# Moving eight adaLN groups of a decoder step from the up loops to the down loops of its first feed-forward stage

## The chip, the cores and the metric

The kernel runs on one core of one Trainium2 chip. The metric is the device time of one execution in microseconds (us), as the median of several runs.

## The reference

One inference step of a one-layer decoder trunk in fp32, for 256 prompt tokens and 8 sample tokens (264 columns in all). Nine modulation vectors of 2048 come from `silu(c) @ w_ada + b_ada`, and the layer is

```
mod = silu(c) @ w_ada + b_ada                       # sh1, sc1, gt1, shm, scm, gtm, sh2, sc2, gt2
h = h + 0.5 * gt1 * swiglu(modulate(h, norm_ffn1, sh1, sc1), w_ffn1_up, w_ffn1_down)
y = mixer(modulate(h, norm_mix, shm, scm))          # gated DeltaNet and dilated window attention
h = h + gtm * y
h = h + 0.5 * gt2 * swiglu(modulate(h, norm_ffn2, sh2, sc2), w_ffn2_up, w_ffn2_down)
return rmsnorm(h, norm_final)
swiglu(x, up, down) = (silu(x @ up[:, :FF]) * (x @ up[:, FF:])) @ down      # FF = 5632
modulate(h, gain, sh, sc) = rmsnorm(h, gain) * (1 + sc) + sh
```

## The kernel before

All weights are streamed once from memory in panels of 128 partitions. An up, qkv or adaLN panel holds 16 tiles of 128x128 (1 MB); a down panel holds 11 (704 KB). SP issues one load after another into a ring of four buffers, `raw` (RAW = 4); before each it waits for `slot_done` of that slot (line 570). A weight panel goes through three engines: ScalarE copies it to `whi` in the fp32r format (`split_hi`, line 696), VectorE subtracts to get `wlo` (`split_lo`, line 1082) and so frees the slot, and PE multiplies whi with the high and the low part of the activations and wlo with the high part (`panel`, lines 1675, 1676, 1683), 48 matmuls for an up panel and 33 for a down panel. whi and wlo have two buffers each (SPLIT = 2).

An adaLN panel is not split. PE reads it from `raw` in plain fp32 (`ada`, line 1733), four matmuls that use 32 columns of the array each, and frees the slot itself when it is through. Four such panels make a group: their sum stands in bank 2 of `mp`, ScalarE copies it to `arow` (`copy_rows`, line 720), PE turns it by four small matmuls (`fold`, line 1743), and VectorE adds the bias and stores four tiles of `mod` (`take_ada`, line 1099). There are 36 groups. The first eight (sh1, sc1) come ahead of everything; the next twelve (gt1, shm, scm) ride in the first feed-forward stage, six in the qkv stage, and the rest later.

The feed-forward stage has two halves of 22 hidden tiles. Each half has an up loop of 44 panels and then a down loop of 4 rounds of 8 panels, which add to `h` (`take_sublayer`, lines 1190 to 1197). In the second half each pair of down panels is followed by a square on ScalarE and a sum on PE (line 1760) for the next norm. The order of the panels in a round is written out by hand in a tuple, in which None stands for an adaLN panel:

```
PLAIN = (0, 1, 2, 3)
MIXED = (0, 1, None, None, 2, None, None, 3)
WIDE = (0, 1, None, 2, 3, None, 4, 5, None, 6, None, 7)
FF1_PLAN = ((WIDE, 5), (MIXED, 1))
FF2_PLANS = ((WIDE, 4), (PLAIN, 3)), ((PLAIN, UP_IT),)
```

SP, ScalarE, VectorE and PE each walk the same plan with their own loop (`ffn` on each of them), so the order of the loads in SP's queue is the order in which PE uses them. The very first two panels of the stage are run together (`duo`, lines 1700 to 1702), as the normed tiles become ready. `set_gate` multiplies gt1 by 0.5 before the first down loop and waits for a number of taken groups; `norm` of the next stage waits for all of them (line 1146 and on).

Of the kernel before, what the change touches and what calls it, by code (L numbers as in the profile page):

```python
# [26 lines left out]
P = 128  # L27
# [7 lines left out]
HALF = KF // 2  # L35
# [90 lines left out]
WIDE = (0, 1, None, 2, 3, None, 4, 5, None, 6, None, 7)  # L126
FF1_PLAN = ((WIDE, 5), (MIXED, 1))
FF2_PLANS = ((WIDE, 4), (PLAIN, 3)), ((PLAIN, UP_IT),)
G_FF1_HALF = 6
G_FIRST, G_ALL = ADA_FIRST // 4, NADA // 4  # L130
G_QKV = G_FIRST + 2 * G_FF1_HALF
G_PB = G_QKV + CT // 4
# [19 lines left out]
R_FF1 = ADA_FIRST  # L152
R_FF1_HALF = FF_HALF + 4 * G_FF1_HALF
R_QKV = R_FF1 + 2 * R_FF1_HALF
R1 = R_QKV + 8 * QKV_IT - S_BA
# [42 lines left out]
def stretches(plan):  # L198

    p = r = g = 0  # L200
    for body, rounds in plan:
        yield body, rounds, p, r, g
        p, r, g = p + rounds * count(body), r + rounds * len(body), g + rounds * (None in body)


# [15 lines left out]
def build(nc, t):  # L221
    ctx = ExitStack()
    with ctx:
# [341 lines left out]
        def _(sp):  # L565
# [21 lines left out]

            def ffn(r0, up, down, o, plan, g0):
                for body, rounds, p, r, g in stretches(plan):
                    with sp.Fori(0, rounds) as i:  # L590
                        body_loads(body, r0 + r, up, UP * o + p, g0 + g, i)
                rd = r0 + sum(len(body) * rounds for body, rounds in plan)
                with sp.Fori(0, 4) as i:
                    for k in range(8):
                        load(seq(rd + k, 8, i), down[i * 8 + (FF_DOWN * o + k)], DOWN * P)

            for o in range(2):
                ffn(R_FF1 + o * R_FF1_HALF, t["up1"], t["down1"], o, FF1_PLAN, G_FIRST + o * G_FF1_HALF)
            with sp.Fori(0, QKV_IT) as i:
# [87 lines left out]
        def _(act):  # L687
# [83 lines left out]

            def ffn(n, o, s0, r0, a0, plan, g0, last):
                for body, rounds, p, r, g in stretches(plan):
                    per, raws = count(body), len(body)
                    with act.Fori(0, rounds) as i:
                        for u in range(per // 2):
                            s = seq(s0 + p + 2 * u, per, i)
                            a = seq(a0 + p + 2 * u, per, i)
                            done(s)
                            act.activation(sg[:, u % 2, :], acc[:, a.slot(BANKS), 0:NT], ACT.Silu)\  # L780
                               .then_inc(acc_taken[a.slot(BANKS)], 1)
                            split_hi(s + 2, seq(r0 + r + spot(body, 2 * u + 2), raws, i))
                            if None in body and u == per // 2 - 1:
                                copy_rows(seq(g0 + g, 1, i), seq(r0 + r + last_ada(body), raws, i))
                            split_hi(s + 3, seq(r0 + r + spot(body, 2 * u + 3), raws, i))
# [5 lines left out]
                shift = r0 + sum(len(body) * rounds for body, rounds in plan) - sd  # L791

                q0, t0 = (N_SQ + KD, T_FF2 + KD) if n else (KD, T_FF1 + KD)

                def down(i, k):
                    split_hi(seq(sd + 2 + k, 8, i), shift, DOWN * P if k < 6 else PANEL)

                if o:
                    ready_root()
                with act.Fori(0, 3 if last else 4) as i:  # L800
                    for k in range(8):
                        down(i, k)
                        if o and k % 2:
# [30 lines left out]
            for o in range(2):  # L834
                ffn(0, o, S_FF1 + o * FF_HALF, R_FF1 + o * R_FF1_HALF, A_FF1 + o * A_FF_HALF,
                    FF1_PLAN, G_FIRST + o * G_FF1_HALF, False)
            norm(1, SHM)
# [236 lines left out]
        def _(dve):  # L1074
# [123 lines left out]

            def ffn(n, o, s0, r0, a0, plan, g0, last, gt):
                for body, rounds, p, r, g in stretches(plan):  # L1200
                    per, raws = count(body), len(body)
                    with dve.Fori(0, rounds) as i:
                        for u in range(per // 2):
                            s = seq(s0 + p + 2 * u, per, i)
                            a = seq(a0 + p + 2 * u, per, i)
                            split_lo(s + 2, seq(r0 + r + spot(body, 2 * u + 2), raws, i))
# [6 lines left out]
                            split_lo(s + 3, seq(r0 + r + spot(body, 2 * u + 3), raws, i))  # L1213
# [8 lines left out]
                shift = r0 + sum(len(body) * rounds for body, rounds in plan) - sd  # L1222
                t0 = (T_FF2 if n else T_FF1) + o * KD
                if o == 0:
                    own_taken(ad - 1)
                    set_gate(gt, 0.5, G_ALL if n else G_FIRST + G_FF1_HALF)

                def down(i, stop):
                    for q in range(4):
                        for k in range(2):  # L1230
                            if k:
                                take_sublayer(seq(sd + 2 * q + 1, 8, i), seq(ad + q, 4, i), q, i, 4, t0)
                            if not (stop and q == 3):
                                split_lo(seq(sd + 2 + 2 * q + k, 8, i), shift, DOWN * P if q < 3 else PANEL)

# [18 lines left out]
            for o in range(2):  # L1254
                ffn(0, o, S_FF1 + o * FF_HALF, R_FF1 + o * R_FF1_HALF, A_FF1 + o * A_FF_HALF,
                    FF1_PLAN, G_FIRST + o * G_FF1_HALF, False, GT1)
            norm(1, SHM, SCM)
# [398 lines left out]
        def _(pe):  # L1656
# [121 lines left out]

            def ffn(n, o, s0, r0, a0, plan, g0, ready=None):
                for body, rounds, p, r, g in stretches(plan):  # L1780
# [7 lines left out]
                sd, ad = s0 + UP, a0 + UP  # L1788
                shift = r0 + sum(len(body) * rounds for body, rounds in plan) - sd
                q0 = N_SQ + KD if n else KD  # L1790

                def down(i, first=False):
                    for q in range(4):
                        s, a = seq(sd + 2 * q, 8, i), seq(ad + q, 4, i)
                        fresh(a)
                        panel(s, shift, [(to(a), us[0:DOWN], True, False)])
                        if o and not (first and q == 0):
                            tile_sum(sq, q0, q - 1, i, first=first and q == 1)
                        panel(s + 1, shift, [(to(a), us[DOWN:HALF], False, True)])

# [16 lines left out]
            for o in range(2):  # L1817
                ffn(0, o, S_FF1 + o * FF_HALF, R_FF1 + o * R_FF1_HALF, A_FF1 + o * A_FF_HALF,
                    FF1_PLAN, G_FIRST + o * G_FF1_HALF, None if o else lambda k: NB * (k // 4) + k % 4 + 2)
            panels(MIXED, S_QKV, R_QKV, A_QKV, G_QKV, 0, lambda k: N_FIRST + k + 2)  # L1820
# [477 lines left out]
```

## Time and profile before

| | us |
|---|---|
| median of 3 runs (2983.6 to 2986.86) | 2985.5 |
| profiled execution, its own time | 2983.18 |
| its span, first to last instruction | 2981.2 |
| PE busy | 2795.1 |
| VectorE (DVE) busy | 1380.1 |
| ScalarE (ACT) busy | 1050.9 |

Durations are read from the one profiled execution. PE is the matmul row of TensorE and PEld its weight loads, which overlap. Matmuls are pipelined, so a single row's duration (0.28 us) is longer than the step from one start to the next (0.12 us). The first stage's up loops run from about 109 to 404 and from about 546 to 830 us of the span, its down loops from there to about 546 and 971 us.

### The profile page before, as it was taken

To read this page: it belongs to the slowest core of one execution; us is meant where nothing else is said; L and a number is where in the kernel's file an instruction comes from. 1 tells how busy PE (TensorE), PEld (TensorE's weight loads), DVE (VectorE), ACT (ScalarE), POOL (GpSimd) and SP (SyncE) were. 2 spreads that over 40 slices of the span, in tenths; PEclk is the share of its full clock that TensorE was granted. 3 is DMA by queue.
4 is the path that set the end of the run, shared out by engine and by line. 5 is a ranking of instruction groups with operands and counts; after the bars stand their busy time and mean duration, and the time that the engine had idled before them with its cause. 6 is when DMAs were issued, how large, how long until landed. Compare 5 with 4: busy or idle time off the path is not lost.

```text
span 2981.2 us, 52107 instructions
## 1 busy us (share of the span) xinstructions
PE 2795.1 (94%) x21861; PEld 2581.8 (87%) x21861; DVE 1380.1 (46%) x1714; ACT 1050.9 (35%) x1067; POOL 12.5 (0%) x32
## 2 busy tenths in 40 slices
PE   5799999999999898999996999979899999999998
PEld 2599989999999787899974999757699999999998
DVE  0444345434344665555555555343443445544444
ACT  1333333333334323433312444222343333333332
POOL 0000000000000000000000000000000000000000
PEclk8899999999999899999987999989899999999999
DMA  9665655656655676333324454766556545554443
GB/s 390 276 245 228 253 190 181 243 225 246 240 182 186 234 284 244 111 126 119 124 86 188 145 180 151 267 235 232 219 228 252 225 144 182 196 183 180 155 159 127
DMA packets 91656, 600.80 MB, mean 202 GB/s; under 512 B 10112, under 2 KB 10240, under 8 KB 32656
## 3 DMA queue, kind: packets, MB, share of 16 engines
q1 hardware_dynamic: 89296, 586.26, 52.8%
q0 software_dynamic: 1808, 11.55, 1.0%
q8 instruction: 97, 1.59, 0.2%
q10 hardware_dynamic: 432, 1.21, 0.1%
q14 instruction: 23, 0.19, 0.0%
HBM read 586.36 MB, written 12.62 MB: 201 GB/s over the span
## 4 chain that ended last, share of the span: by engine, by line
PE 86%; DMA 7%; DVE 3%; ACT 3%; issue 2%; DVEq 0%; ACTq 0%; SPq 0%
PE acc L1675 23%; PE acc L1676 22%; PE acc L1683 21%; PE mp L1733 4%; PE acc L1881 2%; PE acc L1876 2%; PE acc L1875 2%; DMA raw<-in_ada 2%; ACT whi L696 2%; DMA raw<-in_win 2%; DMA raw<-in_wout 1%; DVE wlo L1082 1%; PE mp L1760 1%; PE mp L1947 1%; PE mp L1939 1%
## 5 line engine op out<-in xcount | busy, mean ns | idle before, releaser
L1082 DVE TENSOR_TENSOR wlo<-raw,whi 128x2048 fp32r<-128x2048 f32 (+2 forms) x445 | 929.9, 2090 | 978.2 <-ACT whi L696 977.9
L696 ACT ACTIVATE whi<-raw 128x2048 fp32r<-128x2048 f32 (+2 forms) x445 | 779.2, 1752 | 1015.4 <-PE acc L1683 788.6
L1675 PE MATMUL acc<-xhi,whi 128*128 128x264 f32 x4048 | 1029.1, 291 | 32.5 <-ACT whi L696 32.5
L1676 PE MATMUL acc<-xlo,whi 128*128 128x264 f32 x4048 | 1014.3, 288 | 0.0
L1675 PEld LDWEIGHTS acc<-xhi,whi 128*128 128x128 f32 x4048 | 774.9, 191 | 107.7 <-issue 98.8
L1676 PEld LDWEIGHTS acc<-xlo,whi 128*128 128x128 f32 x4048 | 776.0, 192 | 0.2
L1683 PE MATMUL acc<-xhi,wlo 128*128 128x264 f32 x4048 | 529.8, 284 | 0.0
L1683 PEld LDWEIGHTS acc<-xhi,wlo 128*128 128x128 f32 x4048 | 504.4, 188 | 0.0
L1675 PE MATMUL acc<-uhi,whi 128*128 128x264 f32 x1408 | 360.6, 292 | 17.2 <-DVE ulo L1217 17.2
L1676 PE MATMUL acc<-ulo,whi 128*128 128x264 f32 x1408 | 353.7, 287 | 0.0
L1675 PEld LDWEIGHTS acc<-uhi,whi 128*128 128x128 f32 x1408 | 270.0, 192 | 18.8 <-DVE ulo L1217 17.8
L1676 PEld LDWEIGHTS acc<-ulo,whi 128*128 128x128 f32 x1408 | 270.5, 192 | 1.0
L1733 PE MATMUL mp<-raw,csl 128*32 128x512 f32 x1152 | 165.8, 670 | 34.2 <-DMA par<-in_par 18.9
L1683 PE MATMUL acc<-uhi,wlo 128*128 128x264 f32 x1408 | 192.6, 285 | 0.0
L1683 PEld LDWEIGHTS acc<-uhi,wlo 128*128 128x128 f32 x1408 | 180.5, 189 | 0.0
L780 ACT ACTIVATE sg<-acc 128x264 f32<-128x264 f32 x88 | 34.3, 390 | 370.1 <-PE acc L1683 353.9
L1875 PE MATMUL acc<-xhi,whi 128*128 128x264 f32 x512 | 131.2, 292 | 0.0
L1876 PE MATMUL acc<-xlo,whi 128*128 128x264 f32 x512 | 126.4, 284 | 0.0
L1733 PEld LDWEIGHTS mp<-raw,csl 128*32 128x32 f32 x1152 | 27.3, 115 | 92.4 <-issue 43.6
L1211 DVE TENSOR_TENSOR hf<-sg,acc 128x264 f32<-128x264 f32 x88 | 37.8, 430 | 135.7 <-PE acc L1683 135.7
L1875 PEld LDWEIGHTS acc<-xhi,whi 128*128 128x128 f32 x512 | 96.6, 189 | 0.0
L1876 PEld LDWEIGHTS acc<-xlo,whi 128*128 128x128 f32 x512 | 96.5, 188 | 0.0
(323 smaller groups left out, 1862.7 us busy)
## 6 DMA issues: line engine op xcount, KB each, us to landing
raw<-in_up SPq DMA_DIRECT2D x176, 1024.0 KB, 4.9
raw<-in_ada SPq DMA_DIRECT2D x144, 1024.0 KB, 6.5
raw<-in_down SPq DMA_DIRECT2D x128, 704.0 KB, 4.1
raw<-in_win SPq DMA_DIRECT2D x69, 1024.0 KB, 4.9
raw<-in_wgate SPq DMA_DIRECT2D x32, 1024.0 KB, 4.8
raw<-in_wout SPq DMA_DIRECT2D x16, 1024.0 KB, 7.5
raw<-in_wproj SPq DMA_DIRECT2D x24, 512.0 KB, 5.7
raw<-in_cache SPq DMA_DIRECT2D x12, 1024.0 KB, 6.0
```

The lines of the kernel that those rows point to most:

```text
L696: act.activation(whi[:, s.slot(SPLIT), 0:width], raw[:, r.slot(RAW), 0:width], ACT.Copy)\
L780: act.activation(sg[:, u % 2, :], acc[:, a.slot(BANKS), 0:NT], ACT.Silu)\
L1082: v.tensor_tensor(wlo[:, s.slot(SPLIT), 0:width], raw[:, r.slot(RAW), 0:width], whi[:, s.slot(SPLIT), 0:width].bitcast(F32), ALU.subtract)\
L1211: v.tensor_tensor(hf[:, u % 2, :], sg[:, u % 2, :], acc[:, up, 0:NT], ALU.mult)\
L1675: mm(dst, w, xh, start=starts and k == 0, stop=False)
L1676: mm(dst, w, xl, start=False, stop=False)
L1683: last = mm(dst, wlo[:, b, (tile + k) * P:(tile + k + 1) * P], xh, start=False, stop=ends and k == len(xs) - 1)
L1733: last = mm(mp[QR * j:QR * (j + 1), 2, :], csl[:, QT * p + j, :], raw[:, r.slot(RAW), j * AG:(j + 1) * AG], start=p == 0, stop=p == KD // ...
L1760: mm(mp[:, 0, 0:NT], ones, buf[:, q % 2, :], start=first, stop=last).then_inc(square_summed, 1)
L1875: mm(to(a), w, xh, start=k == 0, stop=False)
L1876: mm(to(a), w, xl, start=False, stop=False)
L1881: last = mm(to(a), wlo[:, b, k * P:(k + 1) * P], xh, start=False, stop=k == KD - 1)
```

## The change

The twelve groups of the stage were spread as six and six over the two up loops. Now four are in the first up loop, in rounds of MIXED at its head, and four in each of the two down loops, one per round, in the order WIDE (its numbers 0 to 7 are then down panels). The rest of the first up loop and all of the second are PLAIN. The gate waits for the first four groups in place of six. Every engine's `ffn` gets the order of the down loop as an argument; without it the order is that of before (DOWNS).

```
+DOWNS = (0, 1, 2, 3, 4, 5, 6, 7)
-FF1_PLAN = ((WIDE, 5), (MIXED, 1))
+FF1_PLANS = ((MIXED, 4), (PLAIN, 7)), ((PLAIN, UP_IT),)
-G_FF1_HALF = 6
+G_FF1 = (0, 8)
+G_FF1_ALL = 12
...
+R_FF1_AT = tuple(R_FF1 + FF_HALF * o + 4 * G_FF1[o] for o in range(2))
...
+def raws(plan):
+    return sum(len(body) * rounds for body, rounds in plan)
+def groups(plan):
+    return sum(rounds for body, rounds in plan if None in body)
 # SP
                 with sp.Fori(0, 4) as i:
-                    for k in range(8):
-                        load(seq(rd + k, 8, i), down[i * 8 + (FF_DOWN * o + k)], DOWN * P)
+                    m = 0
+                    for k, x in enumerate(body):
+                        if x is None:
+                            load(seq(rd + k, len(body), i), t["ada"][i * 4 + (4 * gd + m)])
+                            m += 1
+                        else:
+                            load(seq(rd + k, len(body), i), down[i * 8 + (FF_DOWN * o + x)], DOWN * P)
 # ScalarE
                 def down(i, k):
-                    split_hi(seq(sd + 2 + k, 8, i), shift, DOWN * P if k < 6 else PANEL)
+                    if None in downs and k == 7:
+                        copy_rows(seq(gd, 1, i), seq(rd + last_ada(downs), len(downs), i))
+                    split_hi(seq(sd + 2 + k, 8, i), seq(rd + spot(downs, k + 2), len(downs), i),
+                             DOWN * P if k < 6 else PANEL)
 # VectorE
-                    set_gate(gt, 0.5, G_ALL if n else G_FIRST + G_FF1_HALF)
+                    set_gate(gt, 0.5, G_ALL if n else G_FIRST + 4)
...
+                    if None in downs:
+                        take_ada(gd, i)
 # PE
                 def down(i, first=False):
-                    for q in range(4):
-                        s, a = seq(sd + 2 * q, 8, i), seq(ad + q, 4, i)
-                        fresh(a)
-                        panel(s, shift, [(to(a), us[0:DOWN], True, False)])
-                        if o and not (first and q == 0):
-                            tile_sum(sq, q0, q - 1, i, first=first and q == 1)
-                        panel(s + 1, shift, [(to(a), us[DOWN:HALF], False, True)])
+                    p = 0
+                    for k, x in enumerate(downs):
+                        r = seq(rd + k, len(downs), i)
+                        if x is None:
+                            ada(p, seq(gd, 1, i), r)
+                            p += 1
+                        elif x % 2 == 0:
+                            a = seq(ad + x // 2, 4, i)
+                            fresh(a)
+                            panel(seq(sd + x, 8, i), r, [(to(a), us[0:DOWN], True, False)])
+                            if o and not (first and x == 0):
+                                tile_sum(sq, q0, x // 2 - 1, i, first=first and x == 2)
+                        else:
+                            a = seq(ad + x // 2, 4, i)
+                            panel(seq(sd + x, 8, i), r, [(to(a), us[DOWN:HALF], False, True)])
+                    if p:
+                        fold(seq(gd, 1, i))
```

## Rows read from the trace of the kernel before

**Rows 1.** The page, part 1: busy us, share of the span and instructions by engine.
```profile
PE 2795.1 (94%) x21861; PEld 2581.8 (87%) x21861; DVE 1380.1 (46%) x1714; ACT 1050.9 (35%) x1067; POOL 12.5 (0%) x32
```

**Rows 2.** Windows: stretch, its length, busy time by engine, granted clock, DMA share, rate.
```profile
core 0: us, PE busy (x) PEld busy (x) DVE busy (x) ACT busy (x) POOL busy (x), PEclk, DMA share, GB/s
50.00:100.00 50.00, 36.73 (x205) 11.50 (x204) 16.38 (x50) 15.56 (x30) 0.00 (x0) 0.76 1.00 410
...
122.96:164.53 41.57, 40.55 (x329) 36.73 (x329) 18.62 (x14) 16.29 (x16) 0.00 (x0) 1.00 0.66 253
...
164.53:216.89 52.36, 52.36 (x427) 48.44 (x426) 21.54 (x17) 19.46 (x19) 0.00 (x0) 1.00 0.62 242
...
373.95:404.51 30.56, 28.40 (x234) 25.20 (x233) 10.74 (x9) 9.14 (x10) 0.00 (x0) 1.00 0.64 235
801.39:830.43 29.04, 28.39 (x234) 25.19 (x233) 10.74 (x9) 9.15 (x10) 0.00 (x0) 1.00 0.64 247
1048.03:1077.29 29.26, 28.44 (x234) 25.21 (x234) 17.09 (x30) 8.15 (x6) 0.00 (x0) 1.00 0.75 288
2579.69:2603.07 23.38, 23.38 (x194) 23.38 (x193) 10.72 (x8) 8.84 (x8) 0.00 (x0) 1.00 0.49 179
463.69:495.75 32.06, 32.06 (x266) 32.06 (x265) 17.23 (x20) 12.08 (x8) 0.00 (x0) 1.00 0.54 180
```

**Rows 3.** Timeline of PE: start us, us, instruction, [idle before it <-releaser].
```profile
385.81 1.92 PE L1733 MATMUL mp<-raw,csl 128*32 128x512 f32 x16
...
397.78 0.36 PE L1675 MATMUL acc<-xhi,whi 128*128 128x264 f32 x1 [2.16 <-ACT whi L696]
...
403.71 0.95 PE L1743 MATMUL mp<-con,arow 128*128 128x10 f32 x8
...
415.29 0.28 PE L1675 MATMUL acc<-uhi,whi 128*128 128x264 f32 x1
...
823.72 0.36 PE L1675 MATMUL acc<-xhi,whi 128*128 128x264 f32 x1 [0.65 <-ACT whi L696]
...
829.63 0.95 PE L1743 MATMUL mp<-con,arow 128*128 128x10 f32 x8
...
840.01 0.28 PE L1675 MATMUL acc<-uhi,whi 128*128 128x264 f32 x1
...
1005.02 1.07 PE L1733 MATMUL mp<-raw,csl 128*32 128x512 f32 x8 [1.51 <-DMA raw<-in_ada]
...
1009.62 0.56 PE L1675 MATMUL acc<-xhi,whi 128*128 128x264 f32 x1 [3.53 <-ACT whi L696]
...
2432.47 0.41 PE L1683 MATMUL acc<-xhi,wlo 128*128 128x264 f32 x2
...
2443.58 0.29 PE L1675 MATMUL acc<-uhi,whi 128*128 128x264 f32 x1
...
2825.12 0.28 PE L1683 MATMUL acc<-xhi,wlo 128*128 128x264 f32 x1
...
2836.13 0.29 PE L1675 MATMUL acc<-uhi,whi 128*128 128x264 f32 x1
```

**Rows 4.** The chain of waits at three fourth panels of MIXED: start us, us, what.
```profile
387.79 7.91 DMA raw<-in_up
395.73 1.92 ACT whi L696
...
996.68 10.78 DMA raw<-in_win
...
1032.78 6.41 DMA raw<-in_win
```

**Rows 5.** Timeline of PE after the first stage's duo.
```profile
122.96 1.07 PE L1733 MATMUL mp<-raw,csl 128*32 128x512 f32 x8
125.04 0.36 PE L1675 MATMUL acc<-xhi,whi 128*128 128x264 f32 x1 [1.01 <-ACT whi L696]
```

**Rows 6.** The page, part 6: DMA issues, KB each, median us to landing.
```profile
raw<-in_down SPq DMA_DIRECT2D x128, 704.0 KB, 4.1
```

**Rows 7.** Timelines of DVE, ACT and PE: a take, the norm's start, a down whi.
```profile
408.46 0.19 DVE L1099 TENSOR_TENSOR mod<-mp,par 128x40 f32<-128x40 f32 x1
...
973.12 2.29 DVE L1082 TENSOR_TENSOR wlo<-raw,whi 128x2048 fp32r<-128x2048 f32 x1 [0.99 <-ACT whi L696]
975.33 0.32 DVE L1151 SCALAR_TENSOR_TENSOR gain<-mod,par 128x160 f32<-128x160 f32 x1
975.68 1.80 DVE L1154 RECIPROCAL rs<-srt 128x264 f32<-128x264 f32 x1
...
399.93 0.58 ACT L720 ACTIVATE arow<-mp 128x512 f32<-128x512 f32 x1
...
467.67 1.38 ACT L696 ACTIVATE whi<-raw 128x1408 fp32r<-128x1408 f32 x1 [2.64 <-PE acc L1683]
...
973.45 0.71 PE L1760 MATMUL mp<-sq,con 128*128 128x264 f32 x2 [2.31 <-ACT sq L752]
```

More of the change, by code:

```diff
@@ L126 @@
 WIDE = (0, 1, None, 2, 3, None, 4, 5, None, 6, None, 7)
[L127 removed]
+DOWNS = (0, 1, 2, 3, 4, 5, 6, 7)
+FF1_PLANS = ((MIXED, 4), (PLAIN, 7)), ((PLAIN, UP_IT),)
 FF2_PLANS = ((WIDE, 4), (PLAIN, 3)), ((PLAIN, UP_IT),)
[L129 removed]
+G_FF1 = (0, 8)
+G_FF1_ALL = 12
 G_FIRST, G_ALL = ADA_FIRST // 4, NADA // 4
[L131 removed]
+G_QKV = G_FIRST + G_FF1_ALL
 G_PB = G_QKV + CT // 4
@@ L152 @@
 R_FF1 = ADA_FIRST
-R_FF1_HALF = FF_HALF + 4 * G_FF1_HALF
-R_QKV = R_FF1 + 2 * R_FF1_HALF
+R_FF1_AT = tuple(R_FF1 + FF_HALF * o + 4 * G_FF1[o] for o in range(2))
+R_QKV = R_FF1 + 2 * FF_HALF + 4 * G_FF1_ALL
 R1 = R_QKV + 8 * QKV_IT - S_BA
@@ L586, in body_loads, with ffn @@
                         load(seq(r0 + k, len(body), i), w[i * n + (w0 + x)])
-            def ffn(r0, up, down, o, plan, g0):
-                for body, rounds, p, r, g in stretches(plan):
+            def ffn(r0, up, down, o, plan, g0, body=DOWNS):
+                for b, rounds, p, r, g in stretches(plan):
                     with sp.Fori(0, rounds) as i:
-                        body_loads(body, r0 + r, up, UP * o + p, g0 + g, i)
-                rd = r0 + sum(len(body) * rounds for body, rounds in plan)
+                        body_loads(b, r0 + r, up, UP * o + p, g0 + g, i)
+                rd, gd = r0 + raws(plan), g0 + groups(plan)
                 with sp.Fori(0, 4) as i:
-                    for k in range(8):
-                        load(seq(rd + k, 8, i), down[i * 8 + (FF_DOWN * o + k)], DOWN * P)
+                    m = 0
[5 more added lines that the diff above has]
+                            load(seq(rd + k, len(body), i), down[i * 8 + (FF_DOWN * o + x)], DOWN * P)
             for o in range(2):
-                ffn(R_FF1 + o * R_FF1_HALF, t["up1"], t["down1"], o, FF1_PLAN, G_FIRST + o * G_FF1_HALF)
+                ffn(R_FF1_AT[o], t["up1"], t["down1"], o, FF1_PLANS[o], G_FIRST + G_FF1[o], WIDE)
             with sp.Fori(0, QKV_IT) as i:
@@ L770, in tiles, with ffn @@
                     else bass.ds(i * stride + base, 1)
-            def ffn(n, o, s0, r0, a0, plan, g0, last):
+            def ffn(n, o, s0, r0, a0, plan, g0, last, downs=DOWNS):
                 for body, rounds, p, r, g in stretches(plan):
-                    per, raws = count(body), len(body)
+                    per, turn = count(body), len(body)
                     with act.Fori(0, rounds) as i:
@@ L781, in ffn @@
                                .then_inc(acc_taken[a.slot(BANKS)], 1)
-                            split_hi(s + 2, seq(r0 + r + spot(body, 2 * u + 2), raws, i))
+                            split_hi(s + 2, seq(r0 + r + spot(body, 2 * u + 2), turn, i))
                             if None in body and u == per // 2 - 1:
-                                copy_rows(seq(g0 + g, 1, i), seq(r0 + r + last_ada(body), raws, i))
-                            split_hi(s + 3, seq(r0 + r + spot(body, 2 * u + 3), raws, i))
+                                copy_rows(seq(g0 + g, 1, i), seq(r0 + r + last_ada(body), turn, i))
+                            split_hi(s + 3, seq(r0 + r + spot(body, 2 * u + 3), turn, i))
                             wait_taken(act, a + 1)
@@ L790, in ffn @@
                 sd = s0 + UP
-                shift = r0 + sum(len(body) * rounds for body, rounds in plan) - sd
+                rd, gd = r0 + raws(plan), g0 + groups(plan)
                 q0, t0 = (N_SQ + KD, T_FF2 + KD) if n else (KD, T_FF1 + KD)
                 def down(i, k):
-                    split_hi(seq(sd + 2 + k, 8, i), shift, DOWN * P if k < 6 else PANEL)
+                    if None in downs and k == 7:
+                        copy_rows(seq(gd, 1, i), seq(rd + last_ada(downs), len(downs), i))
+                    split_hi(seq(sd + 2 + k, 8, i), seq(rd + spot(downs, k + 2), len(downs), i),
+                             DOWN * P if k < 6 else PANEL)
                 if o:
@@ L834, in _ @@
             for o in range(2):
-                ffn(0, o, S_FF1 + o * FF_HALF, R_FF1 + o * R_FF1_HALF, A_FF1 + o * A_FF_HALF,
-                    FF1_PLAN, G_FIRST + o * G_FF1_HALF, False)
+                ffn(0, o, S_FF1 + o * FF_HALF, R_FF1_AT[o], A_FF1 + o * A_FF_HALF,
+                    FF1_PLANS[o], G_FIRST + G_FF1[o], False, WIDE)
             norm(1, SHM)
@@ L1197, in take_sublayer, with ffn @@
                 v.tensor_tensor(h[:, m, T:NT], h[:, m, T:NT], ys[:, m, :], ALU.add).then_inc(h_tile, 1)
-            def ffn(n, o, s0, r0, a0, plan, g0, last, gt):
+            def ffn(n, o, s0, r0, a0, plan, g0, last, gt, downs=DOWNS):
                 for body, rounds, p, r, g in stretches(plan):
-                    per, raws = count(body), len(body)
+                    per, turn = count(body), len(body)
                     with dve.Fori(0, rounds) as i:
@@ L1205, in ffn @@
                             a = seq(a0 + p + 2 * u, per, i)
-                            split_lo(s + 2, seq(r0 + r + spot(body, 2 * u + 2), raws, i))
+                            split_lo(s + 2, seq(r0 + r + spot(body, 2 * u + 2), turn, i))
                             done(s + 1)
@@ L1212, in ffn @@
                              .then_inc(acc_taken[up], 1)
-                            split_lo(s + 3, seq(r0 + r + spot(body, 2 * u + 3), raws, i))
+                            split_lo(s + 3, seq(r0 + r + spot(body, 2 * u + 3), turn, i))
                             wait_taken(dve, a + 1)
@@ L1221, in ffn @@
                 sd, ad = s0 + UP, a0 + UP
-                shift = r0 + sum(len(body) * rounds for body, rounds in plan) - sd
+                rd, gd = r0 + raws(plan), g0 + groups(plan)
                 t0 = (T_FF2 if n else T_FF1) + o * KD
@@ L1233, in down @@
                             if not (stop and q == 3):
-                                split_lo(seq(sd + 2 + 2 * q + k, 8, i), shift, DOWN * P if q < 3 else PANEL)
+                                split_lo(seq(sd + 2 + 2 * q + k, 8, i),
+                                         seq(rd + spot(downs, 2 * q + k + 2), len(downs), i),
+                                         DOWN * P if q < 3 else PANEL)
+                    if None in downs:
+                        take_ada(gd, i)
                 with dve.Fori(0, 3 if last else 4) as i:
@@ L1254, in _ @@
             for o in range(2):
-                ffn(0, o, S_FF1 + o * FF_HALF, R_FF1 + o * R_FF1_HALF, A_FF1 + o * A_FF_HALF,
-                    FF1_PLAN, G_FIRST + o * G_FF1_HALF, False, GT1)
+                ffn(0, o, S_FF1 + o * FF_HALF, R_FF1_AT[o], A_FF1 + o * A_FF_HALF,
+                    FF1_PLANS[o], G_FIRST + G_FF1[o], False, GT1, WIDE)
             norm(1, SHM, SCM)
@@ L1777, in panels, with ffn @@
                     fold(g)
-            def ffn(n, o, s0, r0, a0, plan, g0, ready=None):
+            def ffn(n, o, s0, r0, a0, plan, g0, ready=None, downs=DOWNS):
                 for body, rounds, p, r, g in stretches(plan):
@@ L1788, in ffn @@
                 sd, ad = s0 + UP, a0 + UP
-                shift = r0 + sum(len(body) * rounds for body, rounds in plan) - sd
+                rd, gd = r0 + raws(plan), g0 + groups(plan)
                 q0 = N_SQ + KD if n else KD
                 def down(i, first=False):
-                    for q in range(4):
-                        s, a = seq(sd + 2 * q, 8, i), seq(ad + q, 4, i)
-                        fresh(a)
-                        panel(s, shift, [(to(a), us[0:DOWN], True, False)])
-                        if o and not (first and q == 0):
-                            tile_sum(sq, q0, q - 1, i, first=first and q == 1)
-                        panel(s + 1, shift, [(to(a), us[DOWN:HALF], False, True)])
+                    p = 0
[15 more added lines that the diff above has]
+                        fold(seq(gd, 1, i))
                 down(0, True)
@@ L1817, in _ @@
             for o in range(2):
-                ffn(0, o, S_FF1 + o * FF_HALF, R_FF1 + o * R_FF1_HALF, A_FF1 + o * A_FF_HALF,
-                    FF1_PLAN, G_FIRST + o * G_FF1_HALF, None if o else lambda k: NB * (k // 4) + k % 4 + 2)
+                ffn(0, o, S_FF1 + o * FF_HALF, R_FF1_AT[o], A_FF1 + o * A_FF_HALF, FF1_PLANS[o],
+                    G_FIRST + G_FF1[o], None if o else lambda k: NB * (k // 4) + k % 4 + 2, WIDE)
             panels(MIXED, S_QKV, R_QKV, A_QKV, G_QKV, 0, lambda k: N_FIRST + k + 2)
```

## The prediction

> **What bounds the kernel now.** I began with the page's busy shares and the windows, since the change moves work between stages and adds none. TensorE (PE) is busy 2795.1 of 2981.2 us [rows 1]. For the two loops that trade work, the windows give the price of a round. An up round in the order WIDE, eight up panels and four adaLN panels, takes 52.36 us with PE busy 52.36 at a granted clock of 1.00; four plain up panels of the second stage take 23.38, busy 23.38; eight down panels take 32.06, busy 32.06 [rows 2]. So in both places PE is the bound, nothing ends later than it, and no slack exists into which an adaLN panel could vanish. DMA share is 0.62 and 0.54 there, against 410 GB/s moved in the first 100 us, where transfers do bound [rows 2]. Only the order MIXED, with adaLN panels in pairs, has PE idle: 28.40 busy of 30.56, 28.39 of 29.04, 28.44 of 29.26 [rows 2]. The idle stretch sits ahead of the round's fourth weight panel (2.16, 0.65 us) and is released by ScalarE's whi [rows 3]; the chain of waits shows why: that panel's transfer is issued when PE leaves the first pair, lands 6.41 or 7.91 us later, and ScalarE then still needs 1.92 [rows 4]. Meanwhile PE has one panel and one pair of adaLN panels, 5.84 + 1.9 us [rows 3], which is less than 6.41 + 1.92.
>
> **What an adaLN group costs PE.** A plain panel is 23.38 / 4 = 5.845 us. WIDE: 52.36 - 8 x 5.845 = 5.60 us for a group of four and its fold. MIXED: busy 28.4 - 23.38 = 5.02, and 0.65 to 2.16 of waiting. The fold alone is about 0.81 (fold row at 403.71 is 0.95 modelled, the next panel follows 0.81 after a fold's start) [rows 3].
>
> **Removed, half 0 and half 1 of the stage before.** Eleven of the twelve groups stand in steady rounds; the first WIDE round follows the duo, so I take its own stretch, 41.57 us from the duo's end, less six panels (35.07): 6.50 [rows 2]; the excess over 5.60 is the 1.01 wait for the third panel's whi [rows 5]. Nine more WIDE rounds: 9 x 5.60 = 50.40. The two MIXED rounds end at the up loop's end, where the fold lies beside the wait for the last hidden tile; counted up to the fold: 403.71 - 373.95 - 23.38 = 6.38 and 829.63 - 801.39 - 23.38 = 4.86 [rows 2, 3]. Sum 68.14. The joints from there to the second down panel: 415.29 - 403.71 = 11.58 and 840.01 - 829.63 = 10.38 [rows 3]. All together 90.10.
>
> **Added.** (1) Four MIXED rounds at the head of half 0. In the first, both adaLN panels of the pair run after the duo while ScalarE makes the third panel's whi, so that panel starts 2.08 us after the duo (122.96 to 125.04) as it does now with one [rows 5]; then a second pair (half of 5.02 - 0.81, so 2.10), a wait of 0.82 and the fold 0.81: 5.81. The other three are priced at the steady round of the qkv stage, which repeats MIXED with full 1 MB panels: 29.26 - 23.38 = 5.88 each [rows 2], 17.64. (2) Eight groups in the down loops in the order WIDE. No row of before shows an adaLN panel beside a down panel. The nearest is WIDE in the up loop, which has the same breaks in the stream of matmuls: 5.60 each; the lower end is the pairs' 5.02. The last fold of half 1 lies in the 2.31 us in which PE waits for the last square [rows 7], so 8 x 5.60 - 0.81 = 43.99. (3) Both up loops now end in PLAIN, as the second stage's do, where fold start is replaced by the panel's end: from 2432.7 (0.12 after the second of the x2 matmuls of the row at 2432.47 went in) to 2443.58, 10.9 us; in the second stage's other half from 2825.2 to 2836.13, the same [rows 3]. Two joints, 21.8. (4) The last group is now taken by VectorE right before the norm's gain. VectorE is the late one there (wlo at 973.12 for 2.29, gain at 975.33, reciprocal at 975.68), so the take of 0.19 us and a chained step's gap are on the path: 0.35 [rows 7].
> Sum after: 5.81 + 17.64 + 43.99 + 21.8 + 0.35 = 89.6, against 90.10: -0.5 us. On the profiled execution's own 2983.18 us (span 2981.2 and 2.0 around it) that is 2982.7; the median of the runs shown, 2985.5, is 2.3 above that execution, and against it the forecast is 2985.0.
>
> **What else moves, at nothing.** SP issues the same transfers in another order; loads pass each other only inside the ring of four slots. ScalarE gets one more copy of rows (0.58 us) per down round. It stands ahead of the whi of the next round's second panel, which waits for panel 7 anyway (ScalarE idles 2.64 us ahead of such a whi) [rows 7]; if that cover went, the copy would delay whi by 0.6 us, and the panel after it has 2 us to spare. VectorE gets a take of 0.19 per down round. ScalarE is busy 12.08 and VectorE 17.23 of the 32.06 us [rows 2], so both have room. Behind the take are the next round's wlo passes, which wait for a panel of PE anyway. The gate needs only the first four groups, all done in MIXED.
>
> **The place where it could break.** In a down round the adaLN panel at turn 2 frees its slot only when PE has read it, and the load of down panel 4 takes that slot. PE covers it with panels 2 and 3 (2 x 4.01) and one adaLN panel (about 1.2), and ScalarE's whi of 1.38 must fit [rows 2, 7]: 9.2 - 1.4 = 7.8 us. The same holds for panel 6 after the adaLN panel at turn 5: 16 such places in all. A 704 KB panel lands in 4.1 us (median) [rows 6]. Even the slow 7.91 would cost 0.1.
> The trace shows a load landing in 6.41 us with one 1 MB load ahead of it and one behind [rows 4]; three of 1.05 MB sharing 410 GB/s equally would take 7.7. The Trainium skill, "DMA: Bandwidth & Descriptors", section on queues, rings and completion order, says that each DMA engine consumes the descriptors of one ring in ring order: by it panel 4's load is not shared with the two issued behind it; by equal shares it would land in (0.72 + 0.72 + 1.05) / 0.41 = 6.1 us. Neither passes 7.8, so the sum is the same, but the rule is what keeps the next rival small.
>
> **Rivals.** (A) Slower: the down ring. The load of panel 4 or 6 lands later than 7.8 us after its slot is free. For it: 10.78 us was seen once, in the first qkv round [rows 4]. Against it: that round alone shows it, and there POOL's queue copies h out at the same time (line 664), which nothing in a down loop does; the other landings stand at 4.1, 6.41 and 7.91 [rows 4, 6]. At 10.78 it costs 3.0 x 16 = 48 us, so 3033; it decides from 8.2 us on (0.4 x 16 = 6). Chance 0.06. (B) Slower: MIXED rounds wait as the first qkv round did, 1.51 + 3.53 us [rows 3] in place of 0.82: 4 x 4.2 = +17, 3002. For it: half 0's MIXED also stands behind a duo. Against it: the five later qkv rounds wait about what the one in [rows 2] does, 29.26 - 28.44 = 0.82; it passes 6 us from a wait of 2.3 on. Chance 0.04. Its mild form, 2.16 each, adds 4 x 1.34 = 5.4, 2990: chance 0.10, still within the band. (C) Faster: single adaLN panels between short down panels cost no more than in pairs (8 x 0.58 = 4.6 less), the waits of MIXED stay at 0.65 and both joints take the 10.38 of [rows 3]: -4.6 - 0.7 - 1.0 - 0.5 = -6.8, 2978.5. Chance 0.05. (D) My forecast, a swap of equal PE work: 0.75.
>
> **How the numbers follow.** About 0.2%, 6 us, is what a measurement of this kernel can tell from no change. Bounds of the terms: down groups -4.6 to +1.6 (0.1 x 16), MIXED waits -0.7 to +5.4, joints -1.0 to +1.4, norm -0.15 to +0.5; all low gives 2978.5, all high 2993.9. I give 2979 to 2992, in which D and mild B lie; A and B (0.10) stay above. Same: 0.75 + 0.10 = 0.85; faster 0.05; slower 0.10.
>
> **What would show it.** Right: windows over a down round of 37.6 to 37.7 us (32.06 + 5.60) with PE busy throughout and clock 1.00; PLAIN rounds of half 1 at 23.38; MIXED rounds of 29.0 to 29.5; the third panel after the duo at +2.08; gain about 0.35 later behind the last wlo. Wrong: PE idle ahead of down panels 4 and 6 released by whi (A), MIXED rounds above 31 (B), down rounds under 37.2 (C), or a granted clock under 1.00 in the down loops, which no step here allows for.

## The result and the profile after

The changed kernel takes 2993.18 us (median of 10 runs, 2990.63 to 2998.76) against 2984.06 for the kernel before (10 runs, the three shown above among them): a ratio of 1.0032, 95% interval 1.0024 to 1.004, so about 9 us slower. That is far less than 2%, but clear of the noise. Forecast were 2985.0, which is 0.5 under the 2985.5 of the three runs, a range of 2979 to 2992, and "same". The profiled execution took 2996.51 us with a span of 2994.7. A single execution of either kernel scatters over 5 to 10 us, so the two traces are compared by stages.

PE work is unchanged: 2801.5 us busy for the same 21861 matmuls, against 2795.1 [rows 1]; the 6 us more for the same number of matmuls are a first hint of the clock. These are the windows after that answer to [rows 2]: MIXED's first round behind the duo, the next three, a stretch of the second, a down round of each half, four PLAIN panels of each half.

```profile
core 0: us, PE busy (x) PEld busy (x) DVE busy (x) ACT busy (x) POOL busy (x), PEclk, DMA share, GB/s
125.96:143.69 17.73, 15.79 (x129) 12.69 (x129) 7.47 (x5) 6.73 (x7) 0.00 (x0) 1.00 0.86 326
143.69:175.93 32.24, 29.92 (x234) 26.69 (x233) 10.73 (x9) 10.49 (x10) 0.00 (x0) 0.95 0.73 272
175.93:205.21 29.28, 28.43 (x235) 25.20 (x234) 10.73 (x9) 10.53 (x10) 0.00 (x0) 1.00 0.69 265
205.21:234.58 29.37, 28.43 (x235) 25.20 (x233) 10.74 (x9) 10.49 (x10) 0.00 (x0) 1.00 0.75 283
168.50:174.16 5.66, 5.66 (x34) 5.66 (x35) 4.81 (x3) 2.82 (x4) 0.00 (x0) 0.70 0.95 347
442.52:480.32 37.80, 37.80 (x306) 33.89 (x305) 17.34 (x21) 12.60 (x9) 0.00 (x0) 1.00 0.70 264
899.00:938.56 39.56, 39.56 (x314) 35.26 (x313) 17.32 (x21) 13.84 (x13) 0.00 (x0) 1.00 0.67 251
234.58:257.96 23.38, 23.38 (x195) 23.38 (x194) 10.83 (x9) 8.84 (x8) 0.00 (x0) 1.00 0.59 219
556.75:580.13 23.38, 23.38 (x194) 23.38 (x194) 10.39 (x9) 7.92 (x7) 0.00 (x0) 1.00 0.60 217
```

The down rounds and the PLAIN rounds are full: busy equals length at clock 1.00. So the rides in the down loops do not wait anywhere, and a group there costs 37.80 - 8 x 4.013 = 5.70 us (5.60 forecast; 4.013 is 124.41 us between 415.29 and 539.70 before, for 31 down panels; half 1's up loop starts at 540 us there, not at the 546 of the section on the profile before). The losses are in the MIXED rounds. PE's timeline shows the waits; all but the first are at the fourth weight panel:

```profile
128.05 0.36 PE L1699 MATMUL acc<-xhi,whi 128*128 128x264 f32 x1 [0.16 <-ACT whi L713]
...
137.77 0.36 PE L1699 MATMUL acc<-xhi,whi 128*128 128x264 f32 x1 [1.78 <-ACT whi L713]
...
168.50 0.59 PE L1699 MATMUL acc<-xhi,whi 128*128 128x264 f32 x1 [2.32 <-ACT whi L713]
...
169.32 0.42 PE L1700 MATMUL acc<-xlo,whi 128*128 128x264 f32 x1
...
199.27 0.39 PE L1699 MATMUL acc<-xhi,whi 128*128 128x264 f32 x1 [0.85 <-ACT whi L713]
...
228.63 0.39 PE L1699 MATMUL acc<-xhi,whi 128*128 128x264 f32 x1 [0.94 <-ACT whi L713]
```

The third panel behind the duo starts 2.09 us after it, as forecast (2.08). The four waits at fourth panels add to 5.89 us, where four times 0.82, 3.28, were forecast. And behind the wait of 2.32, which follows a pair of adaLN panels, the panel runs at a lower granted clock: steps of 0.22 us between matmuls in place of 0.12 (168.88, 169.10, 169.32), and a mean of 0.70 over that stretch, which is 1.2 GHz for more than half of it. The round's busy time is 29.92 for 28.43, 1.5 us more. With the longer waits this makes up the 27.7 us that the four MIXED rounds cost (273.21 us from the duo's end to the end of the up loop, less 42 panels of 5.845) against 23.45 forecast.

The chain of waits gives the flights of those four loads, the time from issue to landing. Before they were 6.41 and 7.91 us [rows 4]:

```profile
128.09 7.51 DMA raw<-in_up
...
158.49 7.95 DMA raw<-in_up
...
190.73 6.48 DMA raw<-in_up
...
220.00 6.57 DMA raw<-in_up
```

From the first duo's start to the second duo's the first stage takes 876.2 us in this trace, 871.4 before.

### The profile page after: what moved, and what is told of

Read it like the earlier page. It is cut to its first block, busy times and chain, and to the rows that moved or that the text cites. A ratio compares the mean times of both kernels' runs of the same rounds, so it can differ in the third digit from the quotient of the medians.

```text
span 2994.7 us, 52273 instructions
## 1 busy us (share of the span) xinstructions
PE 2801.5 (94%) x21861; PEld 2586.5 (86%) x21861; DVE 1379.5 (46%) x1714; ACT 1049.5 (35%) x1066; POOL 12.5 (0%) x32
## 4 chain that ended last, share of the span: by engine, by line
PE 86%; DMA 7%; DVE 3%; ACT 3%; issue 1%; ACTq 0%; DVEq 0%; SPq 0%
PE acc L1699 23%; PE acc L1700 22%; PE acc L1707 21%; PE mp L1757 4%; PE acc L1915 2%; PE acc L1910 2%; PE acc L1909 2%; ACT whi L713 2%; DMA raw<-in_win 2%; DMA raw<-in_ada 1%; DMA raw<-in_wout 1%; DMA raw<-in_up 1%; DVE wlo L1102 1%; PE mp L1767 1%; PE mp L1784 1%
## 5 line engine op out<-in xcount | busy, mean ns | idle before, releaser
L1757 PEld LDWEIGHTS mp<-raw,csl 128*32 128x32 f32 x1152 | 27.7, 115 | 95.6 <-issue 47.4
```

The costliest lines, as they stand in the source:

```text
L1757: last = mm(mp[QR * j:QR * (j + 1), 2, :], csl[:, QT * p + j, :], raw[:, r.slot(RAW), j * AG:(j + 1) * AG], start=p == 0, stop=p == KD // ...
```

## Experiments

The first eight kernels below were timed in 5 to 11 executions each; the others are a single execution with a trace. Stage is the time from the first duo to the second (the whole first feed-forward stage and the norm behind it), rest is the span less the stage. In the edits, "..." stands for the lines that hand the new order to each engine.

**The MIXED head exchanged for WIDE.**

```
-FF1_PLANS = ((MIXED, 4), (PLAIN, 7)), ((PLAIN, UP_IT),)
+FF1_PLANS = ((WIDE, 4), (PLAIN, 3)), ((PLAIN, UP_IT),)
```

> The changed kernel with the four MIXED rounds at the head of half 0 exchanged for four WIDE rounds (and three PLAIN rounds behind them); the eight groups stay in the down loops. Theory T1, the MIXED rounds at the head are the loss: the head takes 6.5 + 3 x 5.6 = 23.3 us over plain panels in place of the 27.7 traced, so at least 4.4 us less than the changed kernel, and equal to the kernel before within 3 us if the rest of the 9 us is the same waits in worse executions. Theory T2, the rides in the down loops are the loss: still 6 to 9 us over before.

Measured 2988.47 us, ratio 1.0011 (1.0002 to 1.002): 3.3 us over before by the ratio, some 5 under the changed kernel. The stage is 872.6 us. Its first wait is 1.02 and there is no other in the up loop. T2 falls: the rides are all still there. Of the 3.3 us, 1.0 lies in the stage and about 2 in the qkv stage behind it, which takes 185.8 us from the second duo to its last fold for a mean of 183.8 before; the section on the prediction comes back to this.

**Half 1's four groups back in its up loop.**

```
-FF1_PLANS = ((MIXED, 4), (PLAIN, 7)), ((PLAIN, UP_IT),)
+FF1_PLANS = ((MIXED, 4), (PLAIN, 7)), ((WIDE, 4), (PLAIN, 3))
+FF1_DOWNS = WIDE, DOWNS
...
```

> The changed kernel with half 1's four groups moved back from its down loop into its up loop (four WIDE rounds, three PLAIN); half 0 as changed, MIXED head and rides in its down loop. T1: a swap of equal work, 4 x 5.6 for 4 x 5.7 less a hidden fold, so within 1.5 us of the changed kernel and still about 9 over before. T2: half of the loss goes, 4 to 5 us over before.

Measured 2993.59 us, ratio 1.0032 (1.002 to 1.0045), stage 875.6. Undoing half of the rides gives nothing back, as T1 had it.

**All twelve groups in MIXED, none in the down loops.** On the kernel before:

```
-FF1_PLAN = ((WIDE, 5), (MIXED, 1))
+FF1_PLAN = ((MIXED, 6), (PLAIN, 5))
```

> The kernel before with all twelve groups in MIXED rounds in the two up loops (six and five PLAIN in each half), none in the down loops. T1: twelve MIXED rounds at 5.0 us of PE work and 0.85 to 2.3 of waiting, and the clock's fall behind the longest waits, against 68 us now: 2 to 18 us over before, most likely 8; the first two rounds behind the duo cost most. T2: within 3 us of before.

Measured 2995.51 us, ratio 1.0039 (1.0025 to 1.0052), stage 878.8. MIXED alone, with no ride, costs as much as the change did, or a little more (the intervals overlap). Its waits are 0.16, 1.90, 2.14 in the first two rounds and 0.81 to 1.02 in the ten others: the late rounds are nearly as cheap as forecast, the first two are not.

**The changed kernel again.**

> The changed kernel itself once more, for a second trace and time on this chip: 9 us over before (interval 7 to 12). What is open is where the part beyond the 4.7 us between the two duos goes; if MIXED waits vary from execution to execution they differ from 0.16, 1.78, 2.32, 0.85, 0.94 in this trace; if the difference lies in the first 100 us or in the stages after, it stands there again.

Measured 2992.84 us, ratio 1.0031 (1.0019 to 1.0043). Waits 0.16, 2.22, 2.28, 1.04, 1.17; stage 876.2 again. But this trace has no lower clock behind the 2.28, and its rest is 2107.5 against 2118.5 in the first trace.

**MIXED at the end of the up loop.**

```
-FF1_PLANS = ((MIXED, 4), (PLAIN, 7)), ((PLAIN, UP_IT),)
+FF1_PLANS = ((PLAIN, 7), (MIXED, 4)), ((PLAIN, UP_IT),)
```

> The changed kernel with half 0's up loop turned round: seven PLAIN rounds first, then the four MIXED rounds. Theory F (a load that has a 16 KB instruction fetch within its flight lands 1 to 1.5 us later: 7.5 to 8.2 us with one, 6.4 to 6.8 without, in all traces so far; a loop fetches only in its first round, and behind the duo two rounds are new): one of the four waits is 2.0 to 2.4 and three are 0.8 to 1.1, and no panel runs at the lower clock unless behind that one wait; the stage from duo to duo takes 1.5 to 3 us less than the changed kernel's 876.2. Theory P (it is the place next to the duo, where the ring starts empty): all four waits 0.8 to 1.1. If neither: four waits that add to 6 again.

Measured 2990.84 us, ratio 1.0019 (1.001 to 1.0028), stage 874.0, 2.2 less than in the first trace of the changed kernel, within F's 1.5 to 3. But the long wait that F expected is missing: 0.92, 0.78, 1.11, 1.02, which P had. A fetch did fall into the first MIXED round, but it started 2.7 us ahead of the issue of the fourth panel's load and ended before it. So what F says of flights was not put to the test; that the first round of a loop must have a long wait was wrong. PE also waits 2.01 for the third panel behind the duo, since no adaLN panel lies beside ScalarE's whi there.

**The old order in the new code, a null.**

```
-FF1_PLANS = ((MIXED, 4), (PLAIN, 7)), ((PLAIN, UP_IT),)
-G_FF1 = (0, 8)
+FF1_PLANS = ((WIDE, 5), (MIXED, 1)), ((WIDE, 5), (MIXED, 1))
+FF1_DOWNS = DOWNS, DOWNS
+G_FF1 = (0, 6)
...
```

> The changed kernel's code with the order of before (WIDE x5 and MIXED x1 in both up loops, plain down loops): the same instructions in the same order as the kernel before, so a null. Every variant so far lies 2 to 5 us over before beyond its stage's difference. If that is the program's layout or code, this one shows it too, 2 to 5 us over before; if not, it is within 1.5 us of before and the stage takes 871.4 us between the duos.

Measured 2983.18 us, ratio 0.9999 (0.999 to 1.0008), stage 872.0. The rewriting of the functions costs nothing that can be told. The gate waits for six groups here too, as before.

**Pairs with more cover.** MIXED's pairs cost PE less than WIDE's single panels, 5.02 for 5.60 us a group; what MIXED lacks is distance between a pair and the panel that takes its slot.

```
+PAIRS = (0, 1, None, None, 2, 3, 4, 5, None, None, 6, 7)
-FF1_PLANS = ((MIXED, 4), (PLAIN, 7)), ((PLAIN, UP_IT),)
-FF2_PLANS = ((WIDE, 4), (PLAIN, 3)), ((PLAIN, UP_IT),)
+FF1_PLANS = ((PAIRS, 4), (PLAIN, 3)), ((PAIRS, 4), (PLAIN, 3))
+FF2_PLANS = ((PAIRS, 4), (PLAIN, 3)), ((PLAIN, UP_IT),)
+FF1_DOWNS = PAIRS, DOWNS
...
```

> Twelve groups in a new order PAIRS = (0, 1, A, A, 2, 3, 4, 5, A, A, 6, 7): half 0 four in the up loop and four in the down loop, half 1 four in the up loop; the second stage's first up loop uses PAIRS too. A group in pairs costs PE 5.02 against 5.60 in WIDE, and the panel behind a pair's slot has two panels of cover more than in MIXED, so it should not wait. First stage 5.0 + 7 x 5.02 + 4 x 5.13 = 60.7 against 68.1 for before, second stage 2.3 less: 8 to 10 us under before. If the cheap pairs come from MIXED's shape alone and not from pairing, no gain: within 2 us of before.

Measured 2971.03 us, ratio 0.9954 (0.9941 to 0.9968): 13 us under before and 22 under the change. Windows of an up and a down round:

```profile
163.86:215.61 51.75, 51.75 (x427) 48.59 (x425) 21.54 (x17) 19.45 (x18) 0.00 (x0) 1.00 0.65 244
434.03:471.15 37.12, 37.12 (x306) 33.97 (x305) 17.33 (x22) 12.60 (x9) 0.00 (x0) 1.00 0.73 262
```

A group costs 51.75 - 46.76 = 4.99 us, and in the down loop 37.12 - 32.10 = 5.02, with no wait for a panel's whi inside the loops but the 0.16 behind the duo; the stage is 862.5, 9.1 under before. The 13 us are more than the 8 to 10 expected: the part from the output projection's end on, which has PAIRS too, takes 828.5 us for a mean of 831.9 before, 3.4 less where 2.3 was expected.

**The output projection's groups in half 1's down loop too.** On top of the last one: `FF1_DOWNS = PAIRS, PAIRS`, `G_FF1_ALL = 16`, and PLAIN in place of MIXED in the output projection on every engine, with its copies and takes left out there.

> pairs_all with the four groups of the output projection's stage (MIXED there, rounds of about 35 us for 28.4 of PE work) moved into half 1's down loop in PAIRS; the output projection runs PLAIN. If transfers end those rounds: they fall to 23.4 to 25 us, 40 us less, against 4 x 5.1 added in the down loop: 18 to 22 us under pairs_all. If VectorE's and ScalarE's work on the sublayer ends them: rounds stay at 30 or more and the version is no faster than pairs_all.

Measured 2954.07 us, ratio 0.99 (0.9885 to 0.9915): 30 us under before, 39 under the change, and 17 under pairs_all, just short of the 18 to 22 expected. From the last fold ahead of the output projection to the duo behind it, pairs_all and then this kernel:

```profile
1958.04:2142.94 184.90, 149.46 (x1077) 123.92 (x1073) 69.19 (x109) 51.30 (x52) 0.56 (x1) 0.90 0.63 242
```

```profile
1978.02:2122.72 144.70, 121.13 (x917) 116.05 (x913) 69.87 (x105) 48.54 (x48) 0.56 (x1) 0.91 0.52 193
```

40.2 us less there; PE busy falls by 28, its idle time by 12. The stage takes 883.4, 20.9 more. One round of the output projection, pairs_all and then this kernel:

```profile
2063.63:2098.57 34.94, 32.04 (x242) 26.91 (x242) 11.89 (x17) 9.61 (x10) 0.00 (x0) 0.95 0.62 239
```

```profile
2057.11:2082.31 25.20, 25.20 (x202) 24.94 (x201) 12.04 (x16) 8.90 (x9) 0.00 (x0) 1.00 0.47 168
```

Without the adaLN panels a round falls to 25.2 us with PE busy throughout, though VectorE's work stays and ScalarE's falls by 0.7 us only; so these two did not end the rounds. The chain of waits of the round in pairs_all has a load in it, and this kernel has no such wait:

```profile
2078.53 6.36 DMA raw<-in_wout
```

Moving a group away pays where its loads made a transfer end the rounds, which is not so in the first stage.

**Two more traces each of the changed kernel and of the kernel before.**

> The changed kernel, for one more trace. In two traces its first stage takes 876.2 us between the duos (before 871.4), which is 4.8 of about 8.7 us; the other 4 must lie outside it. If they are in the first 100 us, the first duo starts 2 to 3 us later here than in the kernel before's new traces; if in the stages whose rounds a transfer ends (qkv, output projection), the stretches from the second duo to the last qkv fold and over the output projection are 2 us or more longer each; if neither repeats, they stay open.

> As after_look1: first stage 876.2 us; the rest, span less first stage, was 2118.5 and 2107.5 in two traces, so 2107 to 2119 here.

> The kernel before, for one more trace: first stage 871.4 us between the duos; the rest 2109.8 in its one trace and 2112.7 in the null's, so 2105 to 2116 here.

> As before_look1: first stage 871.4 us between the duos, the rest, span less first stage, 2105 to 2116.

The single executions took 2994.02 and 2990.80 us changed, 2983.88 and 2981.23 before. The rests lie in the ranges given; one stage, 874.7 in the first trace after, is 1.5 under the 876.2 expected: it has no slow panel, and its duo is the shortest. With the traces at hand this makes four of the changed kernel and four of the order of before (the null counted in). Means in us; the span's parts in order:

| | before, 4 traces | after, 4 traces | difference |
|---|---|---|---|
| start to the first duo | 109.1 (108.6 to 110.0) | 110.2 (109.0 to 111.5) | 1.1 |
| the stage | 871.6 (871.4 to 872.0) | 875.9 (874.7 to 876.3) | 4.3 |
| second duo to the last qkv fold | 183.8 (183.3 to 184.3) | 185.8 (185.1 to 186.3) | 2.0 |
| from there to the output projection | 800.9 | 800.8 | -0.1 |
| output projection | 184.5 (184.1 to 185.5) | 185.8 (182.1 to 187.8) | 1.3 |
| from there to the end | 831.9 | 831.5 | -0.4 |

The sum is 8.1 of about 9 us. The stage and the qkv part repeat in every trace with no overlap; the first 100 us and the output projection overlap, so they can't be told from scatter. Of the answers expected, the qkv half of the second came true and the rest is open. Inside the stage the duo takes 13.9 to 14.6 us after and 13.5 to 14.4 before, the first part of it at the lower clock; in the mean this is 0.4 of the 4.3, and it may be scatter.

**MIXED behind 2, 3 and 5 PLAIN rounds** (2996.07, 2990.73 and 2992.65 us, one execution each):

```
-FF1_PLANS = ((MIXED, 4), (PLAIN, 7)), ((PLAIN, UP_IT),)
+FF1_PLANS = ((PLAIN, 2), (MIXED, 4), (PLAIN, 5)), ((PLAIN, UP_IT),)    # and 3, 4; and 5, 2
```

> The changed kernel with half 0's up loop as two PLAIN rounds, four MIXED, five PLAIN. Theory F (instruction fetch): for every MIXED round, a wait of 1.8 to 2.4 us if a 16 KB fetch lies within the flight of its fourth panel's load, 0.6 to 1.2 if not; only the first MIXED round can have one. Theory P (place next to the duo): all four waits 0.6 to 1.2 whatever the fetches do.

> As plain_2 with three PLAIN rounds ahead and four behind. F: first MIXED wait 1.8 to 2.4 us if a fetch lies within its load's flight, else 0.6 to 1.2; the others 0.6 to 1.2. P: all four 0.6 to 1.2.

> As plain_2 with five PLAIN rounds ahead and two behind. F: first MIXED wait 1.8 to 2.4 us if a fetch lies within its load's flight, else 0.6 to 1.2; the others 0.6 to 1.2. P: all four 0.6 to 1.2.

All twelve waits in the up loop are 0.85 to 1.33 us and no fetch lies in their flights, so in that loop the three could not separate the theories. But the second qkv round of each has a fetch in flight, a flight of 8.18 or 8.19 us and a wait of 2.56. In eleven of the other 14 traces the same round, at the same place behind the second duo, waits 0.71 to 1.31 us, with no fetch in flight; the waits of 1.70, 1.87 and 2.57 in the last three are among the exceptions below. The stage takes 875.9, 876.1 and 875.5: the short waits gain little here, since the 2.0 us behind the duo are now open, and the two joints between the loops take 22.3 to 22.7 us together for a mean of 21.8 in the changed kernel.

**All flights together.** In 17 traces there are 141 fourth panels of a MIXED round, in the first feed-forward stage and in the qkv stage behind its first round, on which PE waited over 0.3 us. Sorted by whether a 16 KB instruction fetch starts between the issue of the load and its landing:

| | flights | landing, us | PE's wait, us |
|---|---|---|---|
| with a fetch | 19 | 7.51 to 8.19, median 7.91 | 1.78 to 2.56 |
| without | 122 | median 6.55; 117 of them 6.26 to 6.96 | 0.59 to 1.33 in the 117 |
| | | four at 7.33 to 7.43, one at 8.19 | 1.70 to 1.87, and 2.57 |

The one at 8.19 has a fetch that started 0.9 us ahead of the issue and took 1.3; for the four there is none. The first qkv round is left out, since its load lands late in every trace; there it is 11.68 to 12.06 us in the eight traces with a fetch in the flight and 10.65 to 10.84 in the seven with none near (11.30 and 11.75 in the two with one 2 us ahead). DMA queues over the flights at 158.49 and at 190.73 of the changed kernel, in this order:

```profile
DMA packets 389, 2.92 MB, mean 368 GB/s; under 512 B 33, under 2 KB 33, under 8 KB 33
...
q1 hardware_dynamic: 388, 2.91, 95.1%
q8 instruction: 1, 0.02, 0.7%
...
DMA packets 330, 2.44 MB, mean 377 GB/s; under 512 B 32, under 2 KB 32, under 8 KB 32
...
q1 hardware_dynamic: 330, 2.44, 97.6%
```

The rates are alike; the one packet of queue 8 is the difference. The trace also tells where such a packet could act. A load's landing comes as 16 events. In the 19 flights with a fetch the twelfth of them comes at 6.25 to 6.64 us, at 6.43 in the median, and in the 122 without at 6.38: most of the load is as early as ever. Only the last one, two or (once) four events come later than 6.96 us, and a fetch packet takes 0.92 to 0.99 us. So what is late is a small part of the load, about as late as a packet is long or somewhat more. The kernel before holds the cleanest comparison, its own two MIXED rounds: the same panels in the same order, 7.91 us in half 0 with packets of queues 8 and 14 in flight, 6.40 in half 1 with none. The queues over these two flights:

```profile
q1 hardware_dynamic: 424, 2.78, 89.0%
q8 instruction: 1, 0.02, 0.8%
q14 instruction: 1, 0.01, 0.2%
...
q1 hardware_dynamic: 334, 2.36, 94.6%
```

In all four traces of that order the first of these waits is 2.07 to 2.17 and the second 0.59 to 0.76, though the first is 290 us from a duo. So P, the place next to the duo, is not the cause; the fetch goes with it each time. That the fetch delays the load was not tried by itself, since no run places a fetch at will. It is a coincidence seen 19 times of 19, not an intervention, and the four at 7.33 to 7.43 show that something else can make a load late too. The Trainium skill, "Runtime: NRT & Kernel Launch", section "Instruction fetch mechanics", says that each engine's instructions are refilled in blocks of 16 KiB over a DMA queue of its own; the packets of 16384 bytes on queue 8 agree, those of queue 14 have 8192. It does not say that a refill holds up a load.

## Why the prediction was wrong

1. The view of the stage held: outside the MIXED rounds and the joints PE is the bound, rides in the down loops do not wait, and their group costs 5.70 us, forecast 5.60. Both down loops together are 0.7 over the sum (22.72 + 21.95 = 44.67, forecast 43.99).
2. The step that failed is "(1) Four MIXED rounds at the head of half 0", forecast 5.81 + 17.64 = 23.45, traced 27.72, and 27.3 in the mean of four traces. It put each wait for the fourth panel at the 0.82 of one steady qkv round, though [rows 3] had a 2.16 in an up loop, and gave no reason for the two landings, 6.41 and 7.91. The difference repeats: the first two MIXED rounds have a fetch in flight and waits of 1.78 to 2.33 in all six traces with this head, the later ones 0.81 to 1.17. Mild B (2.16 each) stood at 0.10 and 2990; it came for two rounds of four. That the head is what costs was tried: with WIDE in its place the stage falls from 876 to 872.6 us.
3. No term of the head had the clock. The MIXED round of [rows 2] with the wait of 2.16 has 1.00. In four of the six traces with this head the second round's wait (2.14 to 2.32) is followed by a slow panel, 5.5 us for 4.0 up to the wlo pass; in the other two (2.28 and 2.33) it is not.
4. The joints (10.45 + 11.14 = 21.6, forecast 21.8) and the norm (9.50 from the last fold's place to the duo, 9.15 before: forecast 0.35 more) were right. The rows for it, after, to [rows 7]:

```profile
980.27 2.29 DVE L1102 TENSOR_TENSOR wlo<-raw,whi 128x2048 fp32r<-128x2048 f32 x1 [0.99 <-ACT whi L713]
982.48 0.19 DVE L1119 TENSOR_TENSOR mod<-mp,par 128x40 f32 x1
982.81 0.33 DVE L1171 SCALAR_TENSOR_TENSOR gain<-mod,par 128x160 f32<-128x160 f32 x1
983.17 1.80 DVE L1174 RECIPROCAL rs<-srt 128x264 f32<-128x264 f32 x1
```

5. Rival A (the down ring) did not come: no wait for a panel in any down loop. Rival C's mechanism, that pairs are cheaper, is real (4.99 and 5.02 a group), but the change used single panels in the down loops. (Rival C's own sum gives 2985.5 - 6.8 = 2978.7, not 2978.5.) The stated range ended at 2992 though the terms' upper bounds add to 2993.9. The MIXED head alone went 3.9 us over its term, within the 5.4 allowed for it; the sum with the miss of the whole stage, 4.8, gives 2989.8, so what took the time past 2992 lies outside it (6).
6. The sum ended at the second duo. About 2 us more are lost in the qkv stage, whose code and order are the same. There PE waits 2.78, 2.74, 2.70 and 2.75 for the fourth adaLN panel of the first round in the four traces after, and 1.37 to 1.51 in the four of before [rows 3]. In the traces after, a fetch starts 2.3 to 2.6 us before that wait ends, in those of before none is under way. The 13th of the load's 16 landing events comes at 9.1 us after and at 8.9 to 9.1 before; only the last is late. The other kernels agree: the eight traces with a fetch in this flight wait 2.44 to 3.01 there and take 185.1 to 187.5 us for the part, the seven with none near wait 1.37 to 1.57 and take 183.3 to 184.6, half1_ups and mixed_tail among them, which run the changed functions. (all_mixed and out_moved wait 2.47 and 2.17, with a fetch a microsecond ahead of the issue, and take 186.7 and 184.1, so this is not clean either.) The waits of the five rounds behind add to 5.4 us after and 4.2 before; three of the four flights of 7.33 to 7.43 are among them. Landing of that panel by the DMA issues, after and then before:

```profile
raw<-in_ada SPq DMA_DIRECT2D x1, 1024.0 KB, 10.4
```

```profile
raw<-in_ada SPq DMA_DIRECT2D x1, 1024.0 KB, 9.2
```

The order in front has changed where fetches fall in a stage that nobody touched, and with it the stage's time by one to two microseconds; that it is the fetch that does it is argued from these traces, not tried. The first 100 us (1.1) and the output projection (1.3) stay open: both scatter as much from trace to trace.

So of about 9 us: 4.3 in the stage, against 0.5 less forecast. Of this miss of 4.8 the MIXED head is 3.9, its waits and in two of four traces the clock, the down groups are 0.7, and the duo is 0.4; smaller parts cancel. Then 2.0 in qkv, 0.4 less at the end, and the rest is not settled.

## What to carry to other kernels

Before you price a wait that depends on a transfer, list all its occurrences in the trace, not the steady ones: if landings of one load come in two clusters, look for what is in flight in the dear ones and ask how many of the new places will be of that kind. A narrow filler panel is safest where the load that takes its slot has the most work of PE in front of it; here fillers in pairs cost PE less than single ones (4.99 for 5.60 us a group), and with that distance kept they caused no wait. And move a filler away from where its load is what ends the rounds (the output projection, 17 us); between two loops in which PE is full the place alone gains nothing, and only the order did.

## What was not expected of the hardware

- A 1 MB load on which one 16 KB instruction fetch falls lands 7.51 to 8.19 us after its issue (19 flights), without one 6.26 to 6.96 in 117 of 122. Of its 16 landing events at least twelve are on time, and the last one to four are late.
- A break in the stream of 128x264 matmuls by one adaLN panel costs more than by two in a row: 5.60 us a group in singles, 4.99 in pairs, with PE busy throughout in both.
- Behind waits of 2.14 to 2.32 us that follow adaLN panels the granted clock fell to 1.2 GHz in four traces; behind 2.28 and 2.33 in two others, and behind 2.07 to 2.17 in four traces of the old order and 2.56 in the second qkv round of three others, it did not. So the length of the wait alone does not decide it.
